# Residual stream loaded chunk by chunk on two queues, zero products on TensorE at the start, and three of the eight output chunks finished by ScalarE and GpSimd

## The chip, the core and the metric

The kernel runs on one core of one Trainium2 chip. The metric is the device time in microseconds (us) of one execution; the median of three runs is quoted. Besides, one execution was profiled: the hardware profiler records when every instruction of every engine starts and how long it takes.

## What is computed

Two transformer-like blocks in sequence on a residual stream x of 512 tokens and 1024 features, in float32. Cut to what matters here:

```
def first_block(x, ...):
    h = x
    # layer 0: gated short convolution
    h = h + short_conv_mixer(rms_norm(h, a_mix_norm), a_w_in, a_conv, a_w_out)
    h = h + conv_ffn(rms_norm(h, ffn_norm[0]), ...)
    # layer 1: latent attention, then a second conv_ffn
    ...
    return rms_norm(h, final_norm)

def second_block(x, ...):
    # modulated norm, three mixers, gated residual, modulated norm, conv_ffn, gated residual
    ...
    x = x + (1.0 + gate2) * ((jax.nn.silu(gate) * val) @ w_down[l])
    return _rmsnorm(x, g_final)

def rms_norm(x, g):
    return x * lax.rsqrt(jnp.mean(x * x, axis=-1) + EPS) * g
```

`short_conv_mixer` begins with `x_n @ w_in`, split in b, c and h; the kernel starts with the columns of c and h.

## The kernel before

The stream lies feature-major in `X`: 128 partitions, 8 chunks (`KD`) of 512 tokens. All matrices are cut into 291 weight tiles of 128 x 1024 float32 (half a megabyte), each with eight 128 x 128 blocks. Every product is taken in three parts: a tile is split in a rounded half `WH` (ScalarE, `hi`, L549) and the rest `WL` (GpSimd, `lo`, L500, or VectorE, `low`, L948, in the up projections: the set `halves`), and the activations likewise in `XH` (ScalarE, L649) and `XL` (VectorE, `lo_half`, L897). `dot` then issues the three matmuls WH by XH (L1461), WH by XL (L1462), WL by XH (L1463), and `wide` does eight chunks of them into one PSUM bank. There are four slots for raw tiles (`RAW`), two for WH and WL (`SPL`), four PSUM banks in turn.

Each engine runs its own program; semaphores tie them. At the start, SP (the DMA queue of SyncE) issues tile 0, X chunks 0 and 1, tile 1, X chunks 4 and 5, tile 2, tile 3 (L449 and L467). ScalarE's queue issues the vector of gains `vec`, X chunks 2 and 3, chunks 6 and 7, the constants and `gsgu` (L539 to L543). ScalarE then computes `hi(0)`, XH of chunks 0 to 3, `hi(1)`, XH of chunks 4 to 7, then the squares of the eight chunks (L655), with `hi(2)` after the fifth. In program order:

```
            for m in range(KD):
                if m % 2 == 0:
                    act.wait_ge(s_in[f"x{m // 2}"], 16)
                nc.scalar.activation(XH[:, m, :], X[:, m, :], ACT.Copy, scale=vcol("a_mix", m)).then_inc(s_xh, 1)
                if m == 3:
                    hi(1)
```

VectorE computes XL of the eight chunks, then adds the squares to `acc` (L886). TensorE does three tiles of `a_ch`, then the sum of squares over partitions (`sum_squares`, L1485), then tile 3. ScalarE takes the root (L575), VectorE the reciprocal (L890) `rb`, which every eviction of PSUM in this stage multiplies by; with four banks, the product of tile 4 waits for the first eviction.

At the end, after the last chunk of the residual (L928), `token_squares` and the root and reciprocal per token follow; `spread` (L1041 on VectorE, L1496 on TensorE) brings the reciprocal to all partitions in bank `ps[4]`; VectorE multiplies the eight chunks by it and by `g_final` (L1439), and SP writes each out as it is done (L489).

Of the kernel before, what the change touches and what calls it, by code (L numbers as in the profile page):

```python
# [20 lines left out]
BF16 = mybir.dt.bfloat16  # L21
ACT = mybir.ActivationFunctionType
ALU = mybir.AluOpType
AX_X = mybir.AxisListType.X

P = 128
D = 1024
KD = D // P
# [20 lines left out]
RAW = 4  # L49
# [58 lines left out]

def halves(t0):

    own = set()
    for name in ("UP0", "UP1", "UP2"):
        own |= set(range(t0[name] + SPL, t0[name] + SPL + 2 * FF))
    return own


def build(nc, w_tiles, ada_tiles, c_in, x_in, vec_in, const_in, rope_in, mask1_in, mask2_in, gsgu_in, wsp_in, pos_in, out):
    T0, M0, DONE_T, DONE_M = schedule()
# [5 lines left out]
    with ctx:  # L124
# [3 lines left out]
        def sem(name):  # L128
            return ctx.enter_context(nc.semaphore(name))
# [8 lines left out]
        gsgu = sb("gsgu", [P, A_W])  # L138
# [99 lines left out]
        MIXED = (ps[7], ps[4])  # L238


        s_in = {n: sem(f"s_in_{n}") for n in ("x0", "x1", "x2", "x3", "c", "vec", "const", "rope", "gsgu", "wsp", "mask", "pos")}
        s_raw = [sem(f"s_raw{i}") for i in range(RAW)]
        s_hi = sem("s_hi")
        s_lo = sem("s_lo")
# [4 lines left out]
        s_ada = sem("s_ada")  # L249
        s_cact = sem("s_cact")  # L250
        s_set = sem("s_set")
        s_sq = sem("s_sq")
        s_acc = sem("s_acc")
        s_sq2 = sem("s_sq2")
# [63 lines left out]
        s_cc = sem("s_cc")  # L318
        s_co = sem("s_co")
        s_fin = sem("s_fin")  # L320
        s_out = sem("s_out")

        block = ctx.enter_context(nc.Block())
# [2 lines left out]
        def vcol(name, i):  # L326

            first = V[name][0]
            return vec[:, first + i:first + i + 1] if isinstance(i, int) else vec[:, bass.ds(i + first, 1)]
# [27 lines left out]
        N_TOK = 2 * (A_W // P) + C_W // P + B_W // P  # L357
        AUX_YA = AUX_2 + N_TOK
        BLOCKS_A = 4 * HEADS

        def pair_half(t, p, half):

# [79 lines left out]
        @block.sync  # L442
        def _(sp):
            def load(t):
                slot = t % RAW
                if t >= RAW:

                    sp.wait_ge(*low_done(t - RAW))
                sp.dma_start(raw[:, slot, :], w_tiles[t]).then_inc(s_raw[slot], 16)  # L449

            def load_ada(n, m):

                if m == 0:
                    sp.wait_ge(s_hl, FF * (n + 1))
                else:
                    sp.wait_ge(s_ada, ADA * (KD * n + m))
                for q in range(ADA):
                    sp.dma_start(ADA_SLOT[q], ada_tiles[ADA * (KD * n + m) + q]).then_inc(s_ada_in[q], 16)

            def load_crow():  # L460
                sp.dma_start(crow, c_in).then_inc(s_in["c"], 16)


            for k in range(RAW):
                load(k)
                if k < 2:
                    sp.dma_start(X[:, 4 * k:4 * k + 2, :], x_in[:, 4 * k:4 * k + 2, :]).then_inc(s_in[f"x{2 * k}"], 16)  # L467
            for t in range(RAW, NT):
                load(t)
                if t == T0["A_OUT"]:  # L470
                    load_crow()
                if t == T0["UP1"] + RAW:

                    sp.wait_ge(s_ol, HEADS)
                    load_crow()
                for n in range(2):
                    down = t - T0[f"DN{n}"]
                    if down == 5:
                        load_ada(n, 0)
                    elif down >= 6 and down % 3 == 0 and down <= 3 * KD:  # L480
                        load_ada(n, down // 3 - 1)
                if t == T0["DN0"] + 3 * KD + 2:

                    sp.wait_ge(s_ada, ADA * KD)
                    for half in range(2):
                        sp.dma_start(trig[:, half, :], rope_in[half]).then_inc(s_in["rope"], 16)
            for m in range(KD):
                sp.wait_ge(s_fin, m + 1)
                sp.dma_start(out[:, m, :], X[:, m, :]).then_inc(s_out, 16)  # L489
            sp.wait_ge(s_out, 16 * KD)  # L490


        @block.gpsimd
        def _(pool):
            def lo(t, k):

                if isinstance(t, int) and t in BY_DVE:
                    return
                pool.wait_ge(s_hi, t + 1)
                nc.gpsimd.tensor_tensor(WL[k % SPL][:, :], raw[:, k, :], f32(WH[k % SPL][:, :]),  # L500
                                        ALU.subtract).then_inc(s_lo, 1)

            def modulated(e):

                for k in range(1, KD, 2):
                    pool.wait_ge(s_xh, KD * e + k + 1)
                    nc.gpsimd.tensor_tensor(XL[:, k, :], MB[k % 4], f32(XH[:, k, :]), ALU.subtract)\
                        .then_inc(s_xlp, 1)

            def lo_tiles(first, end):  # L510

                start = -(-first // RAW) * RAW
                for t in range(first, min(start, end)):
                    lo(t, t % RAW)

                def four(i):
                    for k in range(RAW):
                        lo(i * RAW + (start + k), k)
                rounds = max(0, (end - start) // RAW)
                repeat(pool, rounds, four, peel=rounds)  # L520
                for t in range(start + rounds * RAW, end):
                    lo(t, t % RAW)


            lo_tiles(0, T0["IN2"] + SPL)
            modulated(E_M2)

            pool.wait_ge(s_in["wsp"], 16)
            nc.gpsimd.affine_select(out=WS[:, :, :], in_=WS[:, :, :], compare_op=ALU.is_ge, fill=0.0, base=0,
                                    pattern=[[0, GROUPS], [1, P]], channel_multiplier=-1).then_inc(s_ws, 1)  # L530
            lo_tiles(T0["IN2"] + SPL, T0["UP2"] + SPL)
            modulated(E_F2)
            lo_tiles(T0["UP2"] + SPL, NT)


        @block.scalar
        def _(act):
            ch = Chain(act, s_act)
            act.dma_start(vec[:, 0:V["width"]], vec_in).then_inc(s_in["vec"], 16)  # L539
            for m in (1, 3):  # L540
                act.dma_start(X[:, 2 * m:2 * m + 2, :], x_in[:, 2 * m:2 * m + 2, :]).then_inc(s_in[f"x{m}"], 16)
            act.dma_start(cst[:, :], const_in).then_inc(s_in["const"], 16)
            act.dma_start(gsgu[:, :], gsgu_in).then_inc(s_in["gsgu"], 16)  # L543

# [99 lines left out]
            hi(0)  # L644
            act.wait_ge(s_in["vec"], 16)
            for m in range(KD):
                if m % 2 == 0:
                    act.wait_ge(s_in[f"x{m // 2}"], 16)
                nc.scalar.activation(XH[:, m, :], X[:, m, :], ACT.Copy, scale=vcol("a_mix", m)).then_inc(s_xh, 1)  # L649
                if m == 3:  # L650
                    hi(1)
# [216 lines left out]
            residual("DN2", 3, None, N_END)  # L868
            token_root(N_END)


        @block.vector
        def _(dve):
# [4 lines left out]
            def zero_pads():  # L878
                ch.step(v.memset(TG[:, 0:2], 0.0))
                ch.link(v.memset(TU[:, 0:2], 0.0))  # L880
# [115 lines left out]
                hidden_lo(FF - 1)  # L996


            ch.link(v.memset(acc[:, :], 0.0))
            zero_pads()  # L1000
            for m in range(KD):
                lo_half(XH[:, m, :], XL[:, m, :], X[:, m, :], vcol("a_mix", m), (s_xh, m + 1), s_xl)
            for m in range(KD):
# [432 lines left out]
            token_inverse(N_END)  # L1436
            dve.wait_ge(s_bc, 5)
            for m in range(KD):
                v.scalar_tensor_tensor(X[:, m, :], X[:, m, :], vcol("g_final", m), ps[4][:, :], ALU.mult, ALU.mult)\  # L1439
                    .then_inc(s_fin, 1)  # L1440


        @block.tensor
        def _(pe):
# [20 lines left out]
            def wide(t, M, i=0, per=0, before=None, src=(XH, XL), ready=True):  # L1465

                if ready:
                    tile_ready(t, i, per)
                bank_free(M, i, per)
                for k in range(KD):  # L1470
                    if before:
                        before(k)
                    last = dot(ps[M % 4][:, :], t, k, src[0][:, k, :], src[1][:, k, :], k == 0, k == KD - 1)
                last.then_inc(s_pe, 1)

            def inputs(e):

                if e < E_M2:
                    return lambda k: pe.wait_ge(s_xl, KD * e + k + 1)
                return lambda k: pe.wait_ge(s_xlp, XLP0[e] + k // 2 + 1) if k % 2 else \  # L1480
                    pe.wait_ge(s_xl, XL0[e] + k // 2 + 1)
# [12 lines left out]
            def spread(count, bank, src):  # L1494
                pe.wait_ge(s_dg, count)
                mm(bank[:, :], cc("ones"), src[:, :], start=True, stop=True).then_inc(s_bc, 1)  # L1496


            def a_ch(i):
                start = isinstance(i, int)  # L1500
                for k in range(4):
                    wide(T0["A_CH"] + k, M0["A_CH"] + k, i, 4, inputs(E_A) if start and k == 0 else None)
                    if start and k == 2:
                        pe.wait_ge(s_in["const"], 16)
                        sum_squares(N_A)
# [303 lines left out]
            pe.wait_ge(s_acc, SQ0[N_END + 1])  # L1809
            token_squares(acc, 0)  # L1810
            spread(5, ps[4], RA)

# [111 lines left out]
```

## Time and profile before

| what | us |
|---|---|
| median of 3 runs | 1821.82 (1821.19 to 1825.4) |
| the profiled execution, its own time | 1823.36 |
| its span, first to last instruction | 1821.5 |
| TensorE busy with matmuls | 1759.3 |
| VectorE busy | 1161.5 |
| ScalarE busy | 700.8 |
| GpSimd busy | 400.2 |

Times within the trace count from the start of the span. A busy share says how much of the span an engine had something in work; matmuls overlap each other, so their starts, not their durations, give their rate. The mean granted clock of TensorE over the span was 0.986 of full speed (2.4 GHz).

### The profile page before, as it was taken

To read this page: it belongs to the slowest core of one execution; us is meant where nothing else is said; L and a number is where in the kernel's file an instruction comes from. 1 tells how busy PE (TensorE), PEld (TensorE's weight loads), DVE (VectorE), ACT (ScalarE), POOL (GpSimd) and SP (SyncE) were. 2 spreads that over 40 slices of the span, in tenths; PEclk is the share of its full clock that TensorE was granted. 3 is DMA by queue.
4 is the path that set the end of the run, shared out by engine and by line. 5 is a ranking of instruction groups with operands and counts; after the bars stand their busy time and mean duration, and the time that the engine had idled before them with its cause. 6 is when DMAs were issued, how large, how long until landed. Compare 5 with 4: busy or idle time off the path is not lost.

```text
span 1821.5 us, 22484 instructions
## 1 busy us (share of the span) xinstructions
PE 1759.3 (97%) x7820; PEld 1413.1 (78%) x7820; DVE 1161.5 (64%) x1509; ACT 700.8 (38%) x975; POOL 400.2 (22%) x172
## 2 busy tenths in 40 slices
PE   7999999999999999999999999899999899999997
PEld 6888788888887765878888888687558688888885
DVE  6566777777557765577777666574766677777223
ACT  4223444443224335344444322332564444444221
POOL 3444100002443320310000255434101300000342
PEclk9999999999999999999999999899999899999998
DMA  4332232324663220232322565222101132322331
GB/s 180 103 105 94 96 98 92 102 94 162 211 206 104 70 70 1 70 104 92 101 95 93 172 213 204 95 93 91 37 1 35 62 101 92 101 95 92 105 104 69
DMA packets 52187, 186.84 MB, mean 103 GB/s; under 512 B 5792, under 2 KB 6048, under 8 KB 52000
## 3 DMA queue, kind: packets, MB, share of 16 engines
q1 hardware_dynamic: 50832, 182.47, 29.7%
q10 hardware_dynamic: 1296, 3.58, 0.5%
q8 instruction: 37, 0.61, 0.1%
q14 instruction: 22, 0.18, 0.0%
HBM read 183.94 MB, written 2.10 MB: 102 GB/s over the span
## 4 chain that ended last, share of the span: by engine, by line
PE 90%; DVE 7%; ACT 2%; issue 1%; DMA 0%; POOL 0%; DVEq 0%; SPq 0%; ACTq 0%
PE ps L1461 27%; PE ps L1463 27%; PE ps L1462 27%; PE ps L1624 1%; PE ps L1719 1%; PE ps L1686 1%; DVE rb L890 1%; DVE RAB L1073 1%; PE ps L1631 1%; DVE stat L1149 1%; PE ps L1707 1%; DVE QXL L897 0%; PE ps L1650 0%; PE ps L1709 0%; PE ps L1726 0%
## 5 line engine op out<-in xcount | busy, mean ns | idle before, releaser
L500 POOL TENSOR_TENSOR WL<-raw,WH 128x1024 fp32r<-128x1024 f32 x159 | 389.2, 2448 | 1375.1 <-ACT WH L549 1375.1
L1461 PE MATMUL ps<-XH,WH 128*128 128x512 f32 x1560 | 614.6, 394 | 18.2 <-DVE XL L897 9.6
L1462 PE MATMUL ps<-XL,WH 128*128 128x512 f32 x1560 | 609.8, 391 | 0.0
L1463 PE MATMUL ps<-XH,WL 128*128 128x512 f32 x1560 | 609.7, 391 | 0.0
L549 ACT ACTIVATE WH<-raw 128x1024 fp32r<-128x1024 f32 x291 | 308.4, 1060 | 580.6 <-PE ps L1463 578.2
L1461 PEld LDWEIGHTS ps<-XH,WH 128*128 128x128 f32 x1560 | 294.4, 189 | 86.9 <-POOL WL L500 9.6
L1462 PEld LDWEIGHTS ps<-XL,WH 128*128 128x128 f32 x1560 | 294.5, 189 | 61.5 <-issue 1.0
L1463 PEld LDWEIGHTS ps<-XH,WL 128*128 128x128 f32 x1560 | 294.4, 189 | 61.6
L1461 PE MATMUL ps<-HH,WH 128*128 128x512 f32 x528 | 205.5, 389 | 0.0
L1462 PE MATMUL ps<-HL,WH 128*128 128x512 f32 x528 | 205.5, 389 | 0.0
L1463 PE MATMUL ps<-HH,WL 128*128 128x512 f32 x528 | 205.4, 389 | 0.0
L948 DVE TENSOR_TENSOR WL<-raw,WH 128x1024 fp32r<-128x1024 f32 x132 | 161.5, 1223 | 30.4 <-ACT WH L549 30.4
L617 ACT ACTIVATE HH<-CU 128x512 f32 (+1 forms) x66 | 41.8, 633 | 207.9 <-DVE CU L990 135.6
L1461 PEld LDWEIGHTS ps<-HH,WH 128*128 128x128 f32 x528 | 99.1, 188 | 21.0 <-issue 0.3
L1462 PEld LDWEIGHTS ps<-HL,WH 128*128 128x128 f32 x528 | 99.1, 188 | 20.6
L1463 PEld LDWEIGHTS ps<-HH,WL 128*128 128x128 f32 x528 | 99.1, 188 | 20.5
L886 DVE TENSOR_TENSOR acc<-acc,SQ 128x512 f32<-128x512 f32 x62 | 84.6, 1365 | 24.9 <-ACT SQ L594 19.5
L897 DVE SCALAR_TENSOR_TENSOR XL<-X,vec,XH (+1 forms) x32 | 56.8, 1789 | 36.7 <-ACT XH L592 27.6
L928 DVE SCALAR_TENSOR_TENSOR X<-ps,gm,X 128x512 f32 x16 | 12.0, 751 | 101.4 <-PE ps L1463 101.4
L924 DVE TENSOR_TENSOR X<-ps,X 128x512 f32 x32 | 22.1, 692 | 82.8 <-PE ps L1463 82.8
L960 DVE TENSOR_TENSOR TU<-ps,rb 128x512 f32<-128x512 f32 x44 | 30.4, 692 | 59.0 <-PE ps L1463 59.0
L628 ACT ACTIVATE CG<-CG 128x512 f32<-128x512 f32 x44 | 27.8, 632 | 99.3 <-DVE CG L970 99.3
(245 smaller groups left out, 1911.5 us busy)
## 6 DMA issues: line engine op xcount, KB each, us to landing
raw<-w_tiles SPq DMA_DIRECT2D x291, 512.0 KB, 3.2
ada<-ada_tiles SPq DMA_DIRECT2D x32, 512.0 KB, 5.4
trig<-ada_tiles SPq DMA_DIRECT2D x16, 512.0 KB, 7.0
out_x<-X SPq DMA_DIRECT2D x8, 256.0 KB, 2.0
X<-x_in SPq DMA_DIRECT2D x2, 512.0 KB, 8.5
X<-x_in ACTq DMA_DIRECT2D x2, 512.0 KB, 8.2
RAB<-c_in SPq DMA_DIRECT2D x2, 512.0 KB, 4.9
MK<-mask_in ACTq DMA_DIRECT2D x1, 1024.0 KB, 5.0
```

Source lines behind the costliest of these rows:

```text
L500: nc.gpsimd.tensor_tensor(WL[k % SPL][:, :], raw[:, k, :], f32(WH[k % SPL][:, :]), ALU.subtract).then_inc(s_lo, 1)
L549: nc.scalar.activation(WH[t % SPL][:, :], raw[:, slot, :], ACT.Copy).then_inc(s_hi, 1)
L617: nc.scalar.activation(at(HH, jj), CU[:, :], ACT.Copy).then_inc(s_hh, 1)
L628: nc.scalar.activation(CG[:, :], CG[:, :], ACT.Silu, bias=vcol("conv_b", jj) if bias else 0.0)\
L886: v.tensor_tensor(acc[:, :], acc[:, :], SQ[:, k % 2, :], ALU.add).then_inc(s_acc, 1)
L897: v.scalar_tensor_tensor(dst_l, src, g, f32(dst_h), ALU.mult, ALU.subtract).then_inc(sem_l, 1)
L924: ins = v.tensor_tensor(at(X, m), bank, at(X, m), ALU.add)
L948: v.tensor_tensor(WL[t % SPL][:, :], raw[:, t % RAW, :], f32(WH[t % SPL][:, :]), ALU.subtract).then_inc(s_lov, 1)
L960: ins = v.tensor_tensor(pad[:, 2:S + 2], ps[M % 4][:, :], rb[:, :], ALU.mult)
L1461: mm(bank, h, xh, start=first, stop=False)
L1462: mm(bank, h, xl, start=False, stop=False)
L1463: return mm(bank, lo, xh, start=False, stop=last)
```

## The change

1. The eight chunks of X are loaded by eight transfers, each with its own semaphore: SP's queue takes tile 0 and then chunks 1, 3, 5, 7 before tiles 1 to 3; ScalarE's queue takes `vec` and then chunks 0, 2, 4, 6 before the constants. ScalarE waits per chunk. `hi(1)` keeps its place after the fourth XH.
2. Tile 0 joins the set `halves`: VectorE computes WL(0), before its first XL, and GpSimd skips it. `a_ch` therefore waits per tile with written-out semaphore values.
3. VectorE fills `rbl` with zeros first, and TensorE multiplies these zeros 14 times, 384 bfloat16 columns each, into `ps[7]`, before its first real product.
4. At the end ScalarE scales chunks 5, 6 and 7 (`BY_POOL`) by `g_final` in place, `spread` is run a second time into `ps[7]`, ScalarE copies that to `rb` in SBUF, and GpSimd multiplies the three chunks by it. VectorE does the other five. SP writes out in the order 0, 1, 2, 5, 3, 6, 4, 7.

```
-    own = set()
+    own = {0}
...
-            for k in range(RAW):
+            load(0)
+            for m in (1, 3, 5, 7):
+                sp.dma_start(X[:, m, :], x_in[:, m, :]).then_inc(s_in[f"x{m}"], 16)
+            for k in range(1, RAW):
                 load(k)
-                if k < 2:
-                    sp.dma_start(X[:, 4 * k:4 * k + 2, :], x_in[:, 4 * k:4 * k + 2, :]).then_inc(s_in[f"x{2 * k}"], 16)
...
-            for m in range(KD):
-                sp.wait_ge(s_fin, m + 1)
+            for m in DONE_ORDER:
+                if m in BY_POOL:
+                    sp.wait_ge(s_fin_pool, BY_POOL.index(m) + 1)
+                else:
+                    sp.wait_ge(s_fin, m + 1 - sum(p < m for p in BY_POOL))
                 sp.dma_start(out[:, m, :], X[:, m, :]).then_inc(s_out, 16)
...
+            pool.wait_ge(s_scaled, len(BY_POOL))
+            pool.wait_ge(s_rsb, 1)
+            for m in BY_POOL:
+                nc.gpsimd.tensor_tensor(X[:, m, :], X[:, m, :], rb[:, :], ALU.mult).then_inc(s_fin_pool, 1)
...
-            for m in (1, 3):
-                act.dma_start(X[:, 2 * m:2 * m + 2, :], x_in[:, 2 * m:2 * m + 2, :]).then_inc(s_in[f"x{m}"], 16)
+            for m in (0, 2, 4, 6):
+                act.dma_start(X[:, m, :], x_in[:, m, :]).then_inc(s_in[f"x{m}"], 16)
...
-                if m % 2 == 0:
-                    act.wait_ge(s_in[f"x{m // 2}"], 16)
+                act.wait_ge(s_in[f"x{m}"], 16)
...
+            for m in BY_POOL:
+                nc.scalar.activation(X[:, m, :], X[:, m, :], ACT.Copy, scale=vcol("g_final", m)).then_inc(s_scaled, 1)
+            act.wait_ge(s_bc, 6)
+            nc.scalar.activation(rb[:, :], ps[7][:, :], ACT.Copy).then_inc(s_rsb, 1)
...
+            v.memset(rbl[:, :], 0.0).then_inc(s_zero, 1)
             ch.link(v.memset(acc[:, :], 0.0))
             zero_pads()
+            low(0, 0)
...
+                if m not in BY_POOL:
+                    v.scalar_tensor_tensor(X[:, m, :], X[:, m, :], vcol("g_final", m), ps[4][:, :], ALU.mult, ALU.mult)\
+                        .then_inc(s_fin, 1)
...
+            pe.wait_ge(s_zero, 1)
+            zeros = rbl[:, :].bitcast(BF16)
+            for _ in range(14):
+                mm(ps[7][:, 0:3 * P], zeros[:, 0:P], zeros[:, 0:3 * P], start=True, stop=True)
+
             def a_ch(i):
                 start = isinstance(i, int)
                 for k in range(4):
-                    wide(T0["A_CH"] + k, M0["A_CH"] + k, i, 4, inputs(E_A) if start and k == 0 else None)
+                    if start:
+                        tile_ready(T0["A_CH"] + k)
+                    else:
+                        tile_ready(T0["A_CH"] + 4 + k, i - 1, 4)
+                    wide(T0["A_CH"] + k, M0["A_CH"] + k, i, 4, inputs(E_A) if start and k == 0 else None, ready=False)
...
             spread(5, ps[4], RA)
+            spread(5, ps[7], RA)
```

## Rows read from the trace of the kernel before

**Rows 1.** Busy table of the page: busy us, share of the span, instructions.

```profile
PE 1759.3 (97%) x7820; PEld 1413.1 (78%) x7820; DVE 1161.5 (64%) x1509; ACT 700.8 (38%) x975; POOL 400.2 (22%) x172
```

**Rows 2.** The chain of waits, first 60 us: start us, us, what.

```profile
12.52 0.43 PE ps L1461
...
16.01 0.23 PE ps L1461
...
28.94 0.87 PE ps L1485 x2
```

**Rows 3.** SP's issues in the timeline; then DMA issues with us to landing.

```profile
1.72 0.42 SPq L449 DMA_DIRECT2D raw<-w_tiles  x1
2.18 0.76 SPq L467 DMA_DIRECT2D X<-x_in  x1
...
2.98 42.32 SPq L449 DMA_DIRECT2D raw<-w_tiles  x9
...
raw<-w_tiles SPq DMA_DIRECT2D x1, 512.0 KB, 8.7
...
X<-x_in SPq DMA_DIRECT2D x1, 512.0 KB, 10.5
...
raw<-w_tiles SPq DMA_DIRECT2D x1, 512.0 KB, 11.4
```

**Rows 4.** Timeline of ScalarE, first 26 us; in brackets idle before and releaser.

```profile
7.89 2.56 ACT L649 ACTIVATE XH<-X,vec 128x512 fp32r<-128x512 f32 x4 [1.38 <-DMA X<-x_in]
10.43 1.06 ACT L549 ACTIVATE WH<-raw 128x1024 fp32r<-128x1024 f32 x1
12.73 2.56 ACT L649 ACTIVATE XH<-X,vec 128x512 fp32r<-128x512 f32 x4 [1.24 <-DMA X<-x_in]
...
19.24 1.05 ACT L549 ACTIVATE WH<-raw 128x1024 fp32r<-128x1024 f32 x1
```

**Rows 5.** Timeline of VectorE and GpSimd, 8 to 26 us.

```profile
8.72 2.75 DVE L897 SCALAR_TENSOR_TENSOR XL<-X,vec,XH 128x512 fp32r<-128x512 f32 x4 [7.09 <-ACT XH L649]
...
11.56 2.38 POOL L500 TENSOR_TENSOR WL<-raw,WH 128x1024 fp32r<-128x1024 f32 x1 [2.63 <-ACT WH L549]
...
13.49 2.99 DVE L897 SCALAR_TENSOR_TENSOR XL<-X,vec,XH 128x512 fp32r<-128x512 f32 x4 [2.02 <-ACT XH L649]
...
20.84 4.06 DVE L886 TENSOR_TENSOR acc<-acc,SQ 128x512 f32<-128x512 f32 x3 [0.57 <-ACT SQ L655]
```

**Rows 6.** Timeline of TensorE: first product, and first product of tile 1.

```profile
9.62 0.76 PE L1461 MATMUL ps<-XH,WH 128*128 128x512 f32 x1 [9.62 <-DVE XL L897]
...
17.89 0.39 PE L1461 MATMUL ps<-XH,WH 128*128 128x512 f32 x1
```

**Rows 7.** Windows around a pause: stretch, us, busy (count) by engine, clock, DMA share, GB/s.

```profile
573.30:576.30 3.00, 0.03 (x1) 0.00 (x0) 2.03 (x4) 1.64 (x3) 0.00 (x0) 0.82 0.16 66
576.30:582.30 6.00, 5.99 (x13) 4.04 (x14) 5.84 (x6) 0.86 (x2) 2.35 (x1) 0.52 0.29 91
```

**Rows 8.** Timeline near 1793 us; then line 928's durations (ns min/median/max).

```profile
1793.02 2.39 POOL L500 TENSOR_TENSOR WL<-raw,WH 128x1024 fp32r<-128x1024 f32 x1 [1.69 <-ACT WH L549]
...
1793.60 2.35 DVE L886 TENSOR_TENSOR acc<-acc,SQ 128x512 f32<-128x512 f32 x1 [0.75 <-ACT SQ L594]
...
L928 DVE SCALAR_TENSOR_TENSOR X<-ps,gm,X x16: 750/751/751, 1393.7 to 1807.1; 128x512 f32 x16
```

**Rows 9.** Tail: timeline; lines L507 and L489 (durations, landing); group L711.

```profile
1811.65 2.08 PE L1496 MATMUL ps<-RAB,cst 128*128 128x512 f32 x2 [1.29 <-DVE RAB L1041]
1813.76 5.36 DVE L1439 SCALAR_TENSOR_TENSOR X<-X,vec,ps 128x512 f32<-128x512 f32 x8 [2.17 <-PE ps L1496]
...
L507 POOL TENSOR_TENSOR XL<-SQ,XH x8: 1275/1280/1297, 1153.8 to 1450.9; 128x512 fp32r<-128x512 f32 x8
...
DMA to landing us min/median/max: 2.0/2.0/2.1
...
L711 ACT ACTIVATE VT<-ps 128x512 f32<-128x512 f32 x8 | 4.8, 596 | 15.3 <-PE ps L1567 15.3
```

More of the change, by code:

```diff
@@ L238, in build @@
         MIXED = (ps[7], ps[4])
-        s_in = {n: sem(f"s_in_{n}") for n in ("x0", "x1", "x2", "x3", "c", "vec", "const", "rope", "gsgu", "wsp", "mask", "pos")}
+        s_in = {n: sem(f"s_in_{n}") for n in ("x0", "x1", "x2", "x3", "x4", "x5", "x6", "x7", "c", "vec", "const", "rope", "gsgu", "wsp", "mask", "pos")}
         s_raw = [sem(f"s_raw{i}") for i in range(RAW)]
@@ L251, in build @@
         s_set = sem("s_set")
+        s_zero = sem("s_zero")
+        s_scaled = sem("s_scaled")
+        s_rsb = sem("s_rsb")
         s_sq = sem("s_sq")
@@ L320, in build @@
         s_fin = sem("s_fin")
+        s_fin_pool = sem("s_fin_pool")
         s_out = sem("s_out")
@@ L359, in build @@
         BLOCKS_A = 4 * HEADS
+        BY_POOL = (5, 6, 7)
+        DONE_ORDER = (0, 1, 2, 5, 3, 6, 4, 7)
         def pair_half(t, p, half):
@@ L1438, in _ @@
             for m in range(KD):
-                v.scalar_tensor_tensor(X[:, m, :], X[:, m, :], vcol("g_final", m), ps[4][:, :], ALU.mult, ALU.mult)\
-                    .then_inc(s_fin, 1)
+                if m not in BY_POOL:
+                    v.scalar_tensor_tensor(X[:, m, :], X[:, m, :], vcol("g_final", m), ps[4][:, :], ALU.mult, ALU.mult)\
+                        .then_inc(s_fin, 1)
         @block.tensor
```

## The prediction

> **What bounds the kernel now.** I read the page's busy table first: TensorE is busy 97% of the span [rows 1], and in the stationary middle nothing in the change touches it. So only the first 36 us and the last 15 us can move. Then I read the chain of waits at the start [rows 2], each engine's timeline there [rows 4 to 6], the DMA issues [rows 3], and the same at the tail [rows 9].
>
> Start. The first weight tile's 24 products need WH(0), WL(0) and, chunk by chunk, XH and XL. XH(0..3) are made by ScalarE from 7.89, hi(1) follows at once at 10.43, and XH(4) waits for SP's second half-megabyte of X until 12.73 [rows 4]. VectorE starts XL(4) at 13.49 and has all four at 16.48 [rows 5]. TensorE crosses into tile 1 at 17.89 [rows 6]. From there it never waits up to the sum of squares at 28.94 [rows 2]; the last addition to acc ends at 20.84 + 4.06 = 24.90 [rows 5], four microseconds early. The root, reciprocal and first evictions hang behind that product, so whatever shifts tile 0's end shifts the whole kernel. Products are 0.43 us apart at 12.5 and 0.23 apart at 16.0 [rows 2]: the start runs at the lower clock level (1.2 GHz), though the granted-clock column has no lower value there; I trust the spacing.
>
> Tail. After the last residual chunk: norm, one spread product (2.08 us), eight VectorE products from 1813.76 to 1819.12, last output landing 2.0 to 2.1 after its issue [rows 9].
>
> **The start, step by step.**
>
> *Loads.* Both queues are served side by side. On SP, w1 (issued 1.72) lands 8.7 later at 10.4, X chunks 4 and 5 (issued 2.18) at 12.7, w2 (2.98) at 14.4 [rows 3]. Before X(4,5) lands, SP has moved w0, X, w1, X: 2 MB. Afterwards SP's order is w0, X1, X3, X5, X7, w1: the same 2 MB, with w1 last, and ScalarE's queue carries vec, 1 MB of X and constants as before. So w1 inherits the landing of the old X(4,5): 12.7 instead of 10.4. Bounds: 10.4 (as now) and 14.4 (w2's). I take 12.7, since the bytes ahead of it are equal. X itself lands sooner, its last chunks near 10.5: SP needs 12.7 - 10.4 = 2.3 us for half a megabyte while both queues are full, and w1 is that half megabyte (estimate).
>
> The Trainium skill, "DMA: Bandwidth & Descriptors", section "Issuing engines are not separate DMA queues", says that transfers issued by different engines interleave on the same 16 engines and that a second issuer saves only issue time. By it the second queue gains nothing in landing times; the rows agree, and the sum above doesn't use it.
>
> *ScalarE.* Two more issues at about 0.45 each put its first copies up to 0.9 later; XH(0..3) then run about 7.3 to 9.9, near today's. Nothing pays for that, because the next instruction is hi(1), still placed after XH(3), and it waits for w1. It blocks XH(4..7), whose data are there. hi(1) runs 12.7 to 13.8 (1.06 [rows 4]); XH(4) starts at 13.8, not 12.73.
>
> *The port.* GpSimd starts lo(1) as soon as hi(1) is done: 13.83 to 16.2 (2.38 [rows 5]). XL(4) would start at 14.5 with two SBUF operands. When such an operation meets GpSimd's, it ends about 0.55 after GpSimd does: in the tail an addition started at 1793.60, GpSimd ended at 1795.41, the addition at 1795.95 [rows 8]; today's XL(4) met only the end of lo(1), which is part of why four XL took 2.99 instead of 2.75 [rows 5]. So XL(4) ends at 16.75, XL(5..7) at 0.67 apiece by 18.8, and TensorE's last three products (0.68) end tile 0 at 19.5: 1.6 later than 17.89. If the port did not block, XL(4) would end at 15.2, XL(7) at 17.3 and tile 0 at 18.0: 0.1 late. The Trainium skill, "SBUF — State Buffer", section "SBUF: two separate sides", states that the port pair of VectorE and GpSimd is an exclusive lock held for the whole instruction, and names VectorE operations with two SBUF inputs. By it the loss is the 1.6; the rows say the same.
>
> low(0) on VectorE (estimate 1.2, half of GpSimd's 2.38) ends about 8.5, XL(0) at 9.2, and TensorE starts about 9.45 instead of 9.62 [rows 6]. Worth nothing: XL(4) ends far later. Covered, too, are the memset of rbl (0.5) and the different wait of a_ch. ScalarE's squares follow XH; the hi(2) copy follows the fifth square. Today it ends 3.8 after XL(7) [rows 4, 5]; then at 22.6, and WL(2) at 25.05, when TensorE wants it at 19.5 + 5.45 = 24.95. That costs 0.1 at most, and only at the upper clock.
>
> *Zero products.* 14 of 384 columns at the lower level take 0.43 x 384/512 = 0.32 each, 4.5 us, from about 1.6 to 6.1. Nothing waits for them. But TensorE then idles 3.4 us to 9.45, and in the middle a 3.0 us pause was enough to fall to the lower level, which then held for 6 us of full work [rows 7]. So I expect no gain at 9.45. The new thing is the second pause: TensorE runs k=0..3 (12 products) by 12.3 to 14.6 and waits for XL(4) until 16.8, 2.2 to 4.5 us. A start at the lower level costs 0.20 per product. Bounds: no fall, 0; or 6 us of work low, 14 products, 2.8. I take 11 products, 2.2, because the pause sits across the 3.0 of the row and a low stretch overlaps it in part.
>
> Head: 1.6 + 2.2 = +3.8.
>
> **The tail.** The three scalings by ScalarE (0.7 each) run 1810.7 to 1812.9, hidden under the spread. VectorE's five end near 1817.1. The second spread follows the first at TensorE's rate: four passes of 512 columns at 0.43, 1.7 us, so 1813.73 + 1.7 = 1815.45. ScalarE's copy from PSUM costs 0.6 [rows 9] plus a hand-over: 1816.2. GpSimd's three products have no row of their own; its subtraction of the same shape costs 1.28 [rows 9]. 1816.25 + 3 x 1.28 = 1820.1, against VectorE's 1819.12 now. Bounds: 0.95 each (even) to 1.4. VectorE reads PSUM, and such operations keep 0.750 to 0.751 beside GpSimd's work [rows 8], so no blocking. The output queue takes 5, 6 and 7 in between and only the last counts. Tail: +1.0 (0 to +1.4). SP's waits cover nothing else.
>
> **Sum.** +3.8 + 1.0 = +4.8. The profiled execution took 1823.36 with a span of 1821.5, so 1828.2 with a span of 1826.3. It lay 1.5 above the median 1821.82; to the median the sum adds 1826.6. About 0.3% (5.5 us) is what a measurement of this kernel can tell from no change, so my forecast is no measurable change, on the slow side.
>
> **Rivals.**
> - *Slower by over 0.3%.* TensorE falls in the second pause and stays low for the 6 us that the row shows: 2.8 instead of 2.2, and w1 lands some 0.5 later because X now comes in half as long packets. 1.6 + 0.5 + 2.8 + 1.0 = +5.9, 1827.7. For it: rows 7's stretch. Against: the pause may be 2.2. It decides once w1 lands after 12.8 with a full 6 us low. Chance 0.27.
> - *The pause is harmless.* Level kept: 1.7 + 1.0 = +2.7, 1824.5. Chance 0.2.
> - *hi(1) doesn't wait.* w1 still lands at 10.4, X is all there by 10.5, XH(4) starts at 11.5; but lo(1) runs 11.5 to 13.9, so XL(4) ends at 14.45 as now and tile 0 at 17.2: -0.7 + 1.0, about 1822. The edits then just move idle time. Chance 0.1.
> - *Faster.* As before but with VectorE not blocked (tile 0 at 15.7, -2.2) and GpSimd's products at VectorE's 0.7 (-0.8): 1818.8, still within 0.3%. Beyond that needs something I don't see. Chance 0.03.
>
> The main case holds 0.4. Faster 0.03, same 0.70 (the main case and most of the milder ones), slower 0.27. The range runs from the hi(1) case, less the spread of the runs (0.6), to w1 landing at 14.4 (+1.7 on the sum), where I stop at 1828.6: 1821.3 to 1828.6.
>
> **What would show it.** In the profile after: hi(1) starting near 12.7 behind a DMA of raw, XH(4) near 13.8; XL(4) lasting about 2.2 and ending 0.5 after lo(1); tile 1's first product at 19.5 to 22; spacing 0.43 after 16.8; 14 short bf16 products ending near 6; GpSimd's three products at 1.28 each ending after VectorE's last by 3 us. The prediction is wrong if w1 lands before 11, if the zero products keep the upper level through to 9.45 and the level then holds, or if GpSimd's products take under 1 us.

## The result, and the profile after

The changed kernel takes 1830.02 us (median of 20 runs) against 1824.36 us (20 runs of the kernel before on the same occasions): 5.7 us or 0.31% slower, ratio 1.003 with a 95% interval of 1.0022 to 1.0038 (4.0 to 6.9 us). Two of the 20 runs of the changed kernel took 1994.06 and 3426.9 us at granted clocks of 0.842 and 0.904, and the ratio leaves these two slow runs out; the median of the other 18 is 1829.4, 5.0 us over the kernel before. The median quoted ahead of the prediction, 1821.82, was that of three runs; single runs of the kernel before lie between 1820.7 and 1827.6, and of the changed one between 1824.4 and 1832.3 (the 18). The profiled execution took 1832.29 us, with a span of 1830.6 us.

The chain of waits at the start shows the new order of events (start us, us, what), where [rows 2] had products only:

```profile
3.23 9.89 DMA raw<-w_tiles
13.14 1.06 ACT WH L563
14.20 0.62 ACT XH L662
14.84 2.35 DVE XL L915
17.24 0.50 PE ps L1482
17.74 0.34 PE ps L1483
18.08 0.43 PE ps L1484
...
32.74 0.87 PE ps L1506 x2
```

The chain goes through the transfer of tile 1, which [rows 3] had landed at 10.4, and through hi(1), XH(4) and one XL of 2.35 us. The sum of squares over partitions starts at 32.74 instead of 28.94.

SP's issues after, and how long the transfer issued at 3.23 took to land:

```profile
1.24 1.94 SPq L472 DMA_DIRECT2D X<-x_in  x4
3.23 28.05 SPq L455 DMA_DIRECT2D raw<-w_tiles  x7
...
raw<-w_tiles SPq DMA_DIRECT2D x1, 512.0 KB, 9.9
```

The timelines of ScalarE, VectorE and GpSimd after, which answer to [rows 4] and [rows 5]:

```profile
7.68 2.59 ACT L662 ACTIVATE XH<-X,vec 128x512 fp32r<-128x512 f32 x4 [0.88 <-DMA X<-x_in]
13.14 1.06 ACT L563 ACTIVATE WH<-raw 128x1024 fp32r<-128x1024 f32 x1 [2.87 <-DMA raw<-w_tiles]
14.10 2.54 ACT L662 ACTIVATE XH<-X,vec 128x512 fp32r<-128x512 f32 x4
...
6.91 1.22 DVE L966 TENSOR_TENSOR WL<-raw,WH 128x1024 fp32r<-128x1024 f32 x1 [4.73 <-ACT WH L563]
8.43 2.74 DVE L915 SCALAR_TENSOR_TENSOR XL<-X,vec,XH 128x512 fp32r<-128x512 f32 x4 [0.30 <-ACT XH L662]
14.84 4.33 DVE L915 SCALAR_TENSOR_TENSOR XL<-X,vec,XH 128x512 fp32r<-128x512 f32 x4 [3.67 <-ACT XH L662]
...
14.28 2.36 POOL L510 TENSOR_TENSOR WL<-raw,WH 128x1024 fp32r<-128x1024 f32 x1 [13.77 <-ACT WH L563]
```

ScalarE stands idle for 2.87 us in front of hi(1), and the wait is for tile 1; then nothing separates hi(1) from XH(4), so its data were there. VectorE's last four XL take 4.33 instead of 2.99. GpSimd's lo(1) ends at 16.64, and the first of the four at 17.19, 0.55 later.

TensorE after ([rows 6]): the zero products, the last product before the pause, the first after it, the first that is fast again, and the first of tile 1 (21.68 instead of 17.89).

```profile
1.55 4.66 PE L1523 MATMUL ps<-rbl 128*128 128x384 bf16 x14 [1.55 <-DVE rbl L1017]
9.33 0.77 PE L1482 MATMUL ps<-XH,WH 128*128 128x512 f32 x1 [3.12 <-DVE XL L915]
...
14.16 0.47 PE L1484 MATMUL ps<-XH,WL 128*128 128x512 f32 x1
17.24 0.50 PE L1482 MATMUL ps<-XH,WH 128*128 128x512 f32 x1 [2.61 <-DVE XL L915]
...
21.23 0.39 PE L1483 MATMUL ps<-XL,WH 128*128 128x512 f32 x1
21.45 0.39 PE L1484 MATMUL ps<-XH,WL 128*128 128x512 f32 x1
21.68 0.40 PE L1482 MATMUL ps<-XH,WH 128*128 128x512 f32 x1
```

The tail after, which answers to [rows 9]:

```profile
1814.35 0.75 DVE L946 SCALAR_TENSOR_TENSOR X<-ps,gm,X 128x512 f32 x1 [11.10 <-PE ps L1484]
1816.59 1.86 PE L1511 MATMUL ps<-cst,acc 128*128 128x1 f32 x8 [2.51 <-DVE acc L904]
...
1819.75 3.77 PE L1517 MATMUL ps<-RAB,cst 128*128 128x512 f32 x4 [1.29 <-DVE RAB L1061]
1821.87 3.38 DVE L1460 SCALAR_TENSOR_TENSOR X<-X,vec,ps 128x512 f32<-128x512 f32 x5 [2.17 <-PE ps L1517]
1823.56 0.60 ACT L887 ACTIVATE rb<-ps 128x512 f32<-128x512 f32 x1 [2.97 <-PE ps L1517]
1824.30 3.71 POOL L547 TENSOR_TENSOR X<-X,rb 128x512 f32<-128x512 f32 x3 [16.16 <-ACT rb L887]
```

VectorE is done with its five at 1825.25, GpSimd with its three at 1828.01.

To compare traces I cut each in three at two instructions that every kernel has: the **head** runs to the start of the sum of squares over partitions (28.94 before, 32.74 after), the **middle** from there to the start of the last residual operation (1778.1 and 1781.6), the **tail** from there to the end of the span (14.5 and 16.2). The two traces differ by 3.8 + 3.5 + 1.7 = 9.0 us, more than the medians' 5.7, so one pair of traces is not the answer. That is what the experiments are for.

### The profile page after: what moved, and what is told of

Same layout as the page of the kernel before. It is cut to its first block, busy times and chain, and to the rows that moved or that the text cites. A ratio compares the mean times of both kernels' runs of the same rounds, so it can differ in the third digit from the quotient of the medians.

```text
span 1830.6 us, 22526 instructions
## 1 busy us (share of the span) xinstructions
PE 1769.1 (97%) x7836; PEld 1417.6 (77%) x7836; DVE 1162.4 (64%) x1508; ACT 703.5 (38%) x979; POOL 402.7 (22%) x174
## 4 chain that ended last, share of the span: by engine, by line
PE 89%; DVE 6%; ACT 2%; issue 1%; DMA 1%; POOL 0%; SPq 0%; POOLq 0%; DVEq 0%; ACTq 0%
PE ps L1482 27%; PE ps L1483 27%; PE ps L1484 27%; PE ps L1716 1%; PE ps L1654 1%; PE ps L1749 1%; DVE rb L908 1%; DVE RAB L1093 1%; PE ps L1661 1%; PE ps L1737 1%; DMA raw<-w_tiles 1%; DVE stat L1169 1%; PE ps L1517 0%; DVE QXL L915 0%; PE ps L1680 0%
## 5 line engine op out<-in xcount | busy, mean ns | idle before, releaser
L1482 PE MATMUL ps<-XH,WH 128*128 128x512 f32 x1560 | 614.5, 394 | 16.2 <-DVE XL L915 5.7
L915 DVE SCALAR_TENSOR_TENSOR XL<-X,vec,XH (+1 forms) x32 | 58.3, 1837 | 31.6 <-ACT XH L606 27.6
```

The lines of the kernel that those rows point to most:

```text
L915: v.scalar_tensor_tensor(dst_l, src, g, f32(dst_h), ALU.mult, ALU.subtract).then_inc(sem_l, 1)
L1482: mm(bank, h, xh, start=first, stop=False)
```

## The experiments

The three stretches of every trace, in us, with the medians of the timed ones:

| kernel | head | middle | tail | ratio to before, 95% interval |
|---|---|---|---|---|
| before | 28.94 | 1778.1 | 14.5 | |
| e9, f1, f3 (before again) | 28.49, 28.75, 28.49 | 1777.7, 1775.7, 1777.3 | 14.9, 15.0, 14.5 | 1.0003 (0.9994 to 1.0012), e9 |
| after | 32.74 | 1781.6 | 16.2 | 1.003 (1.0022 to 1.0038) |
| e12, f2, f4 (after again) | 34.01, 32.74, 32.74 | 1777.3, 1776.9, 1777.0 | 15.3, 15.2, 15.4 | 1.0046 (1.0033 to 1.0059), e12 |
| e1 head edits only | 33.05 | 1777.0 | 14.5 | 1.0023 (1.001 to 1.0036) |
| e2 tail edits only | 28.57 | 1777.3 | 15.4 | 1.0007 (0.9998 to 1.0016) |
| e3 hi(1) behind XH(7) | 29.04 | 1780.2 | 14.3 | 1.0005 (0.9997 to 1.0014) |
| e4 lo(1) on VectorE | 31.09 | 1777.8 | 15.2 | |
| e5 one zero product | 33.80 | 1780.6 | 14.5 | 1.0035 (1.0019 to 1.0051) |
| e6 zero products in the pause | 31.21 | 1783.8 | 14.5 | 1.0012 (1.0002 to 1.0021) |
| e7 tile 1 loaded earlier | 28.78 | 1781.9 | 14.2 | 1.0011 (1.0001 to 1.0021) |
| e8 best head | 27.12 | 1785.1 | 14.5 | 0.9996 (0.9986 to 1.0005) |
| e10 one chunk for GpSimd | 28.89 | 1778.1 | 14.5 | 1.0004 (0.9995 to 1.0013) |
| e11 best head, one chunk | 26.98 | 1782.7 | 14.5 | 0.9998 (0.9988 to 1.0008) |

**e1, the head edits alone.** The change with all of VectorE's eight final products back:

```
-        BY_POOL = (5, 6, 7)
-        DONE_ORDER = (0, 1, 2, 5, 3, 6, 4, 7)
+        BY_POOL = ()
+        DONE_ORDER = tuple(range(KD))
...
-            spread(5, ps[7], RA)
```

> The change without its tail edits. I read three stretches of each trace: the head up to the start of the sum of squares over partitions on TensorE (28.94 us before, 32.74 after), the middle from there to the last residual operation on VectorE (1778.1 before, 1781.6 after), and the tail from there to the end of the span (14.4 before, 16.3 after). My theory (hi(1) waits for w1, GpSimd's lo(1) then blocks XL(4), TensorE restarts at the lower clock) gives a head of 32.7 with hi(1) at 13.1 and XL(4) ending at 17.2, and a tail of 14.4 to 15.2 as before: 3.8 us slower than before in all. The rival that the loss comes from the tail and the middle, and the head's share is chance of one execution, gives a head near 29 and under 1 us in all.

The head is 33.05, the tail 14.48, and the ratio 1.0023 is most of the change's 1.003. The larger part of the loss is at the start.

**e2, the tail edits alone.** Loads, tile 0, the waits on X and the zero products as before.

> The change without its head edits (loads, tile 0 on VectorE, zero products all as before). My theory gives a head of 28.9 and a tail 1.0 longer than before's: the second spread ends 1.7 after the first, GpSimd's three products follow at 1.24 each, and the last output is issued 1.0 later than VectorE alone would have it. In all +1.0 us. The rival that the tail costs 1.8, as the two traces differ there, expects +1.8; I put the other 0.8 down to the lower clock during the token squares (1.86 against 1.05), which is not the edit's. A middle that differs by 2 or 3 us in either direction speaks for chance there.

The head is 28.57. The tail is 15.43, 0.94 over before, at equal token squares (1.05):

```profile
1808.11 1.05 PE L1509 MATMUL ps<-cst,acc 128*128 128x1 f32 x8 [2.50 <-DVE acc L904]
...
1812.57 3.38 DVE L1458 SCALAR_TENSOR_TENSOR X<-X,vec,ps 128x512 f32<-128x512 f32 x5 [2.17 <-PE ps L1515]
...
1815.02 3.71 POOL L546 TENSOR_TENSOR X<-X,rb 128x512 f32<-128x512 f32 x3 [15.36 <-ACT rb L887]
```

So the other 0.8 us of the first trace's tail is its slower token squares (1.86 against 1.05), which no other trace of the tail edits repeats (tails of 15.2 to 15.4). The edits don't cause it either: the same operation took 1.83 in e4, 1.50 in e9 and 1.56 in f1, which all end as the kernel before does.

**e3, hi(1) behind the eighth XH.** As e1, and:

```
             for m in range(KD):
                 act.wait_ge(s_in[f"x{m}"], 16)
                 nc.scalar.activation(XH[:, m, :], X[:, m, :], ACT.Copy, scale=vcol("a_mix", m)).then_inc(s_xh, 1)
-                if m == 3:
-                    hi(1)
+            hi(1)
```

> As e1, but hi(1) moved behind the eighth XH on ScalarE, so nothing waits for w1 before XL is complete. My theory: XH(0..7) run from 7.7 to 12.8 without a gap, XL ends near 14, hi(1) at 13.1 to 14.2, TensorE runs tile 0 from 9.3 without a pause, at the lower level until about 14.7, and enters tile 1 at 17.2 to 17.6 against 21.7; head mark at 28.2 to 28.5 (the token of lo(1) at 16.6 does not delay it). In all -0.5 us against before. The rival that the small transfers, the later table load or tile 0 on VectorE cost the time keeps the head above 30.

Moving one instruction takes the head from 33.05 to 29.04. The expected 28.2 to 28.5 was missed by half a microsecond: lo(1) now fell on the first additions to acc, hi(2) waits for the fifth square, and tile 2 began 0.15 late; most of the rest is the product rate, which rose only at 15.2.

**e4, lo(1) on VectorE.** As e1, hi(1) where the change has it:

```
-    own = {0}
+    own = {0, 1}
...
                 lo_half(XH[:, m, :], XL[:, m, :], X[:, m, :], vcol("a_mix", m), (s_xh, m + 1), s_xl)
+            low(1, 0)
```

> As e1 with hi(1) where the change has it, but WL(1) computed by VectorE behind the eighth XL instead of by GpSimd. If GpSimd's lo(1) blocks XL(4), XL(4) now takes 0.74 instead of 2.35 and ends at 15.6, XL(7) at 17.7, WL(1) at 18.9, and TensorE resumes tile 0 at 15.6 instead of 17.2: the pause falls from 2.6 to 1 us. Then the head mark is 1.6 earlier by the block alone (31.1), and up to 3 earlier (29.7) if the shorter pause also keeps the clock up. If the block is not the cause, the mark stays at 32.7.

The chain of waits of e4, at the place where the change has `14.84 2.35 DVE XL L915`:

```profile
13.09 1.06 ACT WH L559
14.15 0.62 ACT XH L658
14.79 0.76 DVE XL L909
15.60 0.62 PE ps L1477
```

The same operation on the same operands takes 0.76 us without GpSimd beside it and 2.35 with it. The Trainium skill ("SBUF — State Buffer", section "SBUF: two separate sides") calls the port pair an exclusive lock; the two numbers agree with that. The head is 31.09, as expected from the block alone. The pause (13.77 to 15.60) was 1.8 us and not the 1 expected, and it did not save the clock: the products behind it are 0.43 apart until 19.0.

**e5, one zero product instead of 14.** As e1, `range(1)` for `range(14)`.

> As e1, with 1 zero product instead of 14. My theory: the level that the zero products reach is lost in the 3.5 us before the first real product at 9.3, so nothing changes: head mark 32.3 to 33.1, first twelve products of tile 0 at 0.43 us. The rival that they help somewhat (as they are meant to) expects a later mark, by up to 2.5 us (35.5). A mark earlier than 32 would say that they harm.

The head is 33.80, over the 32.3 to 33.1 that I expected and 0.75 over e1, but within the 32.74 to 34.01 of the five traces that have the 14. The 0.75 arises behind the pause, where the products stay 0.43 apart for 5.7 us against 3.3 in e1. No gain of the zero products can be seen, and none is excluded below that spread.

**e6, zero products in the pause.** As e1, and in the first tile's wait:

```
+                    def before(k):
+                        if e == E_A and k == 4:
+                            for _ in range(14):
+                                mm(ps[7][:, 0:3 * P], zeros[:, 0:P], zeros[:, 0:3 * P], start=True, stop=True)
+                        pe.wait_ge(s_xl, KD * e + k + 1)
+                    return before
```

> As e1, with 14 more zero products between chunk 3 and chunk 4 of tile 0, where TensorE waits for XL(4). They take 2.2 us at the upper and 4.5 at the lower level. My theory says that the fall in this pause costs about 2.2 of the 3.8: if the level has risen by the pause, it is then kept, XL(4..7) set the pace and the mark falls to 30.6 to 31.3. If the level is still low in the pause, the filling itself overruns the wait by up to 1.8 and the mark stays at 32 to 33.5. The rival that the clock plays no part expects 33 in any case.

The head is 31.21, though TensorE resumes at 17.20, as in the change (17.24). Two windows of e6, and the same of e12, which is the change (stretch, us, busy and count by engine, clock, DMA share, GB/s):

```profile
14.20:17.20 3.00, 1.89 (x12) 0.92 (x11) 2.40 (x2) 3.00 (x6) 2.37 (x1) 1.00 0.89 358
17.20:21.50 4.30, 4.30 (x19) 3.49 (x20) 3.99 (x7) 1.86 (x4) 0.00 (x0) 1.00 0.37 122
```

```profile
14.20:17.20 3.00, 0.01 (x1) 0.01 (x1) 2.40 (x2) 3.00 (x6) 2.35 (x1) 0.89 0.86 348
17.20:21.50 4.30, 4.30 (x10) 3.43 (x11) 3.99 (x7) 1.85 (x4) 0.00 (x0) 0.50 0.39 122
```

With the pause filled the granted clock stays at 1.00 (2.4 GHz) and 19 products are issued in 4.3 us; with it empty the clock is 0.50 (1.2 GHz) and there are 10. e12 is the extreme of the change's traces: the first one has 0.60 and 12 products in the same window. The products stay 0.43 apart for about 3.3 us in that trace, in f2, f4 and e1, and for 6.1 us in e12. The clock's share is thus 33.06 (mean of the five traces with the change's start) less 31.21 = 1.9 us, 1.5 against the three traces at 32.74 and 2.8 against e12.

**e7, tile 1 between X3 and X5.** As e1, and in SP's queue:

```
             for m in (1, 3, 5, 7):
                 sp.dma_start(X[:, m, :], x_in[:, m, :]).then_inc(s_in[f"x{m}"], 16)
+                if m == 3:
+                    load(1)
```

> As e1, but SP's queue is w0, X1, X3, w1, X5, X7, w2, w3: the weight tile lands before the last X chunks, as before the change. Theory (w1's landing gates): hi(1) starts near 10.5, XH(4) at 11.5, lo(1) 11.6 to 14.0 blocks XL(4) until 14.5, no long pause, tile 0 ends at 17.2 to 17.9, head mark 28.2 to 28.9: the whole 3.8 is gone with the order of one transfer. The rival that small transfers or the queues cost time keeps it at 31 or more.

ScalarE, VectorE and GpSimd in e7:

```profile
10.66 1.04 ACT L561 ACTIVATE WH<-raw 128x1024 fp32r<-128x1024 f32 x1
11.61 2.55 ACT L660 ACTIVATE XH<-X,vec 128x512 fp32r<-128x512 f32 x4
...
12.35 4.35 DVE L911 SCALAR_TENSOR_TENSOR XL<-X,vec,XH 128x512 fp32r<-128x512 f32 x4 [0.76 <-ACT XH L660]
...
11.78 2.38 POOL L512 TENSOR_TENSOR WL<-raw,WH 128x1024 fp32r<-128x1024 f32 x1 [11.28 <-ACT WH L561]
```

hi(1) starts 2.5 us earlier and the head is 28.78. The block is still there (the four XL take 4.35), but XL(4) now ends near 14.7, about when it did before the change. So the place of one transfer in the queue decides the whole loss of the head. The third rival of the prediction expected 0.7 less than before from this order; the head is 28.78 against a mean of 28.69 before, so the earlier X gains nothing. The median of e7 is still 0.11% (0.01 to 0.21) above the kernel before, though its head and tail are not: that difference must lie in the middle.

**e8, the best head I could form.** As e3, with lo(1) on VectorE, hi(2) behind the third square and 28 zero products.

> As e3 (hi(1) behind the eighth XH), and besides WL(1) on VectorE behind the eighth XL, hi(2) after the third square instead of the fifth, and 28 zero products instead of 14 to reach nearer to the first real one. Theory: XL(7) ends at 14.4, WL(1) at 15.7, with the upper level kept tile 0 ends at 15.1 and tile 1 starts at 15.75, WL(2) is ready at 20.5 before it is wanted at 21.2; head mark 26.7, 2.2 earlier than before. If the level is low at 9.4 in spite of the zero products, tile 0 ends at 17.4 and the mark is 28.4. In all -0.5 to -2.2 us against before.

The head is 27.12, 0.4 over what I expected and 1.8 under the first trace of before (1.6 under the mean of six); tile 1 starts at 15.93. TensorE had the upper level from 9.36 on (products 0.23 apart). The ratio is 0.9996: with a middle that scatters by more, a gain of this size can't be shown by times.

**e9, the kernel before once more**, and **e12, the change once more**:

> The kernel before itself, once more: a control of what a comparison and a single trace can tell. Head mark 28.5 to 29.3, tail 14.2 to 15.3, ratio 1.000. The question is the middle: all traces run the same instructions there, yet e1 to e8 and the change took 1777.0 to 1785.1, mostly above the 1778.1 of the first trace of before. If that is the phase of the clock's low stretches, this trace may lie anywhere in that band and the ratio is 1. If the new code itself lengthens the middle, this one shows about 1778 again.

> The change itself once more. Head mark 32.7 to 33.8, tail 15.4 at the upper level during the token squares (16.2 only if the level has fallen by then), sum of both 4.7 to 5.9 over before. If the middle's 1781.6 was phase, it lies elsewhere in 1777 to 1785 now, and the ratio is 1.0026 to 1.0035; a middle of 1781.6 again would say that the change reaches into it.

The control came out as it should: head 28.49, tail 14.9, ratio 1.0003. e12's head, 34.01, lies just over the 33.8 that I expected, and its ratio of 1.0046 (1.0033 to 1.0059, six runs against 28) over the 1.0026 to 1.0035: by medians the change cost 7.9 us here and 5.0 in the first measurement.

**f1 to f4**, one trace each of before, the change, before, the change:

> The kernel before, one more trace. So far four traces with the head of before (before, e2, e9, e10) have a middle of 1777.3 to 1778.1, and ten with a changed head have 1777.0 to 1785.1. If the middle's length is the clock's luck in both, this one may exceed 1779; if the changed head reaches into the middle, it stays at 1777 to 1778.5. Head mark 28.5 to 29.3.

> The change, one more trace. Head mark 32.5 to 34.0, tail 15.2 to 16.3. The middle as in f1: luck puts it anywhere in 1777 to 1785, in after and before alike.

> As f1, a second trace: a middle above 1779 in one of the two is enough for scatter in the kernel before too; both at 1777 to 1778.5 make it six of six.

> As f2, a second trace: head mark 32.5 to 34.0, tail 15.2 to 16.3; the mean head mark of the traces of the change then rests on four.

The six traces that start as before have a middle of 1775.7 to 1778.1. Of the change's own four, three have 1776.9 to 1777.3 and the first 1781.6. The extra microseconds of long middles lie mostly between 1263 and 1432, where TensorE runs short products with waits: by the starts of the WH copies, e8 loses 6.8 us on the first trace of before in this stretch, and the first trace of the change 3.4. One stretch of before and the same one of e8 (middle 1785.1):

```profile
1366.00:1383.00 17.00, 15.93 (x96) 12.95 (x95) 13.56 (x30) 9.21 (x14) 0.00 (x0) 1.00 0.00 1
```

```profile
1365.00:1383.00 18.00, 18.00 (x63) 13.20 (x63) 9.70 (x21) 6.91 (x11) 0.00 (x0) 0.53 0.00 0
```

The same code, once at 1.00 with 96 products in 17 us, once at 0.53 with 63 in 18.

The timed executions say more on this than the traces do. Each has a span, and the span less the head and tail of that kernel's traces (43.4 us before) leaves an estimate of its middle. Of 95 executions of the kernel before, 23 have a middle over 1779, and the longest 1782.5 (the one run beside f1 to f4: span 1825.9 at clock 0.983, where the short ones have 0.987 or 0.988). The mean is 1778.0. Of the 54 executions of e3, e6, e7, e8 and e11, 26 are over 1779, and the mean is 1779.5. So the kernel before has long middles too, which the six traces that start like it happened to miss, and they are more frequent behind another start.

**e10, one chunk for ScalarE and GpSimd.** As e2 with `BY_POOL = (7,)`, chunk 7 written out before chunk 6.

> As e2 (only the tail edits), but with one chunk instead of three for ScalarE and GpSimd: BY_POOL = (7,), written out before chunk 6. VectorE's seven products end 0.67 earlier than its eight did; GpSimd's one ends 3.7 + 1.24 after the start of the first spread product's successor, well before. Tail 0.67 shorter than before's: 13.8 at the same clock (e2: 15.43). The rival that handing work to GpSimd costs something in itself at the end expects 14.5 or more.

The tail is 14.46: no gain, and my 13.8 is refuted. The profile says why:

```profile
1811.56 3.78 PE L1515 MATMUL ps<-RAB,cst 128*128 128x512 f32 x4 [1.29 <-DVE RAB L1059]
...
1813.67 4.70 DVE L1458 SCALAR_TENSOR_TENSOR X<-X,vec,ps 128x512 f32<-128x512 f32 x7 [2.17 <-PE ps L1515]
1814.44 4.63 SPq L498 DMA_DIRECT2D out_x<-X  x8
...
1816.12 1.27 POOL L546 TENSOR_TENSOR X<-X,rb 128x512 f32<-128x512 f32 x1 [15.36 <-ACT rb L887]
```

VectorE ends 0.66 earlier and SP issues its last transfer 0.3 earlier (12.10 us after the last residual operation at 1806.97, against 12.42 in the trace of before), but its last transfer takes 2.4 us to land against 2.0, and the span does not end earlier. A window of the kernel before (the last two figures are the DMA engines' share and GB/s):

```profile
1816.00:1818.00 2.00, 0.00 (x0) 0.00 (x0) 2.00 (x4) 0.00 (x0) 0.00 (x0) 0.50 1.03 396
```

and two of e10:

```profile
1816.00:1818.00 2.00, 0.00 (x0) 0.00 (x0) 2.00 (x4) 0.00 (x0) 1.27 (x1) 0.50 1.03 396
1818.00:1820.00 2.00, 0.00 (x0) 0.00 (x0) 0.37 (x1) 0.00 (x0) 0.00 (x0) 0.50 1.05 406
```

The DMA share is 1.03 and over in both. The eight outputs are 2.1 MB, 5.3 us at 396 GB/s, and VectorE's eight products took 5.36: the transfers already kept the pace of the end before, and chunks that are ready sooner only queue. The later landing of the last one agrees with this. That the transfers bound the end is my reading; I have not tried it apart.

**e11, e8's head with e10's tail.**

> The head of e8 with the tail of e10. Head mark 27.1, tail 13.8: 2.5 us under before in these two stretches. The median can be anywhere within 2 of that, since the middle scatters by as much: -0.5 to -4.5.

Head 26.98, tail 14.45 (not 13.8, as in e10), ratio 0.9998 (0.9988 to 1.0008): it beats the change, and can't be told from the kernel before.

## Why the prediction missed

**The step that failed is the last of the sum: "to the median the sum adds 1826.6".** The +4.8 was laid on a median of three runs, 1821.82, and the range on it left only 0.6 for the scatter of the runs, on one side. Twenty runs put the base at 1824.36. The measured 1830.02 is 3.4 above my figure (the 1829.4 of the 18 is 2.8 above); 2.5 of this is the base. On that base my sum gives 1829.2. The base itself moved from one occasion to the next: 24 to 28 runs each gave 1822.93, 1822.32 and 1822.92 beside the experiments. The profiled execution of before, 1823.36, would have given 1828.2.

**"No measurable change" failed with it.** It rested on 5.5 us as the least that could be told from nothing, a bound that I had not measured. The interval of the result is 1.5 us to either side, so 4.8 was well over what twenty runs can tell.

**The size of the difference.** By means over traces, the head costs 33.06 - 28.69 = 4.4 (five and six traces; predicted 3.8), the tail 15.50 - 14.59 = 0.9 (five traces with the change's tail, eleven with before's; predicted 1.0), the middle 1778.0 - 1777.4 = 0.6 (five and six; predicted 0). Together 5.9, inside the measured 4.0 to 6.9 and just under e12's 6.0 to 10.8. The head is the term of the sum that was too small, by 0.6. That the whole came so near is in part luck, since its errors had both signs:

- *Loads.* w1 landed at 13.1, not 12.7. Right in kind (e3, e7), short by 0.4; why it came later than the bytes ahead of it say, these runs don't show. That a second queue adds no bandwidth holds in the trace of before: 412 GB/s from 13 to 14, with both queues at work, and 426 from 15 to 16, with SP's alone.
- *The port.* Right, with its price: XL(4) ended 0.55 after lo(1); e4 took off 1.6 to 2.
- *The clock.* Taken at 2.2; 1.9 by e6 against the mean, and between 1.8 (32.74 - 28.94 less the 2.0 of the two items above) and 3.1 (34.01) from trace to trace. The fall itself came as forecast. So, nearly, did the loss of what the zero products had raised: the first products are 0.43 apart from the second on in most traces, and only after one to three faster ones in e6, e7 and e12.
- *Zero products without gain, low(0) without effect, squares and hi(2) in step.* As forecast; e5 can't exclude a small share.
- *Before's head* was 28.94 in the trace I summed against and 28.69 on average: 0.25 more. With this, the items make 4.1 to 4.2 of the 4.4; the rest has no place.
- *Tail.* The second spread, the copy (0.60) and GpSimd's products (1.24 each) came within 0.1 of their terms. (The bounds of the range hold small slips: +1.7 on 1826.6 is 1828.3 and not 1828.6, and the low end sums to 1821.5 and not 1821.3. Neither changes the outcome.)
- *The rivals.* "Slower by over 0.3%", +5.9 by w1 0.5 late and a full 6 us at the lower level, names the right place, and w1's delay is right. Its long low stretch shows in e12 alone; the other four traces with this start have 3.3 us. Its figure, 1827.7, is too low for the same reason as mine, the base. It had 0.27.

**Open.** The prediction let nothing in the middle move. The change's middles are 0.6 longer by traces, and over the 24 timed executions of the change (the 18 and e12's six) the estimate has a mean of 1779.5 against 1778.0 of the 95 of before; but the twenty runs of before of the first measurement come to 1778.8 in the same way (with 1.8 us between a run's time and its span), so occasions differ by as much as 0.8. Seven traces with other starts (e3 to e8, e11) have middles of 1777.8 to 1785.1, mean 1781.7; the six with before's start stay under 1778.2. Slow clock stretches in the middle occur in the kernel before as well, and more often behind a changed start; by what means a start reaches 1300 us further on, these runs don't show. The longer middles are also why e7, e8 and e11 gained less in the medians than in their heads.

## What to carry to other kernels

When transfers are put in a new order, look at which in-order engine waits for the one that was pushed back, and what is queued behind that wait: X(4) landed near 10.2 (issued 2.2, 8.0 to landing) instead of 12.7 and was used 1.4 us later, because hi(1) stood in front of XH(4). Work given to a second engine at the end must be summed along its own chain (second product, copy, three slow operations), not by the work it takes off the first. And a forecast of five microseconds in 1800 needs a base from more runs than three, or its range must carry the scatter of the base.

## What the runs showed that I had not expected

The untouched middle varied by 9 us, 1775.7 to 1785.1, over eighteen traces of nearly the same instructions; around 1365 to 1383 the clock was low for 18 us in e8 and not at all in before. Six traces with one start looked alike, and only the spans of 95 timed executions showed that this was chance in part. And handing one output chunk to GpSimd freed 0.66 us of VectorE at the very end of the kernel without moving the end, where the transfers ran at 396 to 406 GB/s anyway.
